# Index scores of a sparse attention in six pairs instead of four groups of three

## What is computed

```python
# per layer of the first block, z = h @ w_in + b_in, split into
#   qa, ka, va, qi, ki, wi, qb, kb, vb, ga, gb
qi = partial_rope(qi.reshape(b, s_len, 8, 64), cos, sin)      # index queries, 8 heads
ki = partial_rope(ki.reshape(b, s_len, 1, 64), cos, sin)      # one index key
# per block of 128 queries:
logits = einsum('bqhd,bsd->bqhs', qib, k_idx)
score = einsum('bqh,bqhs->bqs', wb, relu(logits)) * INDEX_SCALE
score = where(admissible, score, -inf)
_, sel = top_k(score, 128)                 # 128 keys are kept for each query
# softmax attention of qa over the chosen ka, va; beside it a banded attention of
# qb (rms-normed), kb (rms-normed), vb; then gates, projections and an FFN
```

## Time and profile before

| | |
|---|---|
| median of three runs | 3193.2 us |
| lowest, highest | 3189.02, 3198.23 us |
| profiled execution, its own time | 3192.15 us |
| its span, first to last instruction | 3190.6 us |
| mean granted TensorE clock, share of full speed | 0.979 |
| busy: TensorE, VectorE, ScalarE, GpSimd | 3015.2, 1709.6, 1261.1, 1094.2 us |
| index scores of layer 0, of layer 1 | from 97.9, from 930.7 us |
| first band score of layer 0, of layer 1 | 149.3, 982.1 us |

### The profile page before, as it was taken

How to read it: one execution, slowest core, us unless ns; L and a number is a source line. 1 busy time by engine, 2 the same in 40 slices (tenths; PEclk the granted TensorE clock), 3 DMA queues, 4 the chain that set the end, 5 groups by cost and what they waited for, 6 DMA issues and landing times.

```text
span 3190.6 us, 36918 instructions
## 1 busy us (share of the span) xinstructions
PE 3015.2 (95%) x13938; PEld 2279.8 (71%) x13938; DVE 1709.6 (54%) x2835; ACT 1261.1 (40%) x1912; POOL 1094.2 (34%) x538
## 2 busy tenths in 40 slices
PE   5999999999989999999998999999999997999998
PEld 2666777888756667788785777877777885666664
DVE  5687664222157868422214454655677136666664
ACT  4355434223245453422323444323334234455543
POOL 1242343444423324344442554444444431000001
PEclk9999999999999999999999999999999998999999
DMA  5112563433321136374232333624442334899995
GB/s 226 53 60 73 173 200 110 147 125 100 114 80 53 57 103 238 116 308 149 91 112 78 115 119 109 194 86 117 137 124 67 93 106 174 340 381 382 381 383 207
DMA packets 188505, 501.25 MB, mean 157 GB/s; under 512 B 20080, under 2 KB 98032, under 8 KB 172224
## 3 DMA queue, kind: packets, MB, share of 16 engines
q1 hardware_dynamic: 165808, 417.24, 38.5%
q0 software_dynamic: 13200, 49.32, 4.0%
q10 hardware_dynamic: 9344, 32.61, 2.9%
HBM read 463.83 MB, written 35.29 MB: 156 GB/s over the span
## 4 chain that ended last, share of the span: by engine, by line
PE 75%; DVE 12%; ACT 4%; DMA 4%; issue 2%; POOL 1%; ACTq 1%; SPq 0%; DVEq 0%; POOLq 0%
PE banks L739 18%; PE banks L740 18%; PE banks L741 18%; PE banks L1451 5%; PE banks L1432 2%; PE banks L1434 2%; PE banks L1433 2%; DMA ring<-in_w_all 2%; PE banks L832 1%; PE banks L853 1%; PE banks L842 1%; DVE abuf L2333 1%; ACT w_hi L1536 1%; PE banks L813 1%; DMA arena<-in_w_all 1%
## 5 line engine op out<-in xcount | busy, mean ns | idle before, releaser
L3012 POOL TENSOR_TENSOR w_lo<-ring,w_hi 128x1024 fp32r<-128x1024 f32 (+1 forms) x375 | 907.3, 2422 | 1385.9 <-ACT w_hi L1536 1385.9
L740 PE MATMUL banks<-h_lo,w_hi 128*128 128x512 f32 x2104 | 827.9, 393 | 0.0
L739 PE MATMUL banks<-hx_hi,w_hi 128*128 128x512 f32 (+2 forms) x1400 | 592.3, 423 | 35.8 <-DVE h_lo L2195 16.3
L1536 ACT ACTIVATE w_hi<-ring 128x1024 fp32r<-128x1024 f32 (+1 forms) x375 | 388.8, 1038 | 551.1 <-DMA ring<-in_w_all 481.5
L741 PE MATMUL banks<-hx_hi,w_lo 128*128 128x512 f32 (+2 forms) x1400 | 553.9, 396 | 0.0
L740 PEld LDWEIGHTS banks<-h_lo,w_hi 128*128 128x128 f32 x2104 | 399.5, 190 | 86.7 <-issue 10.2
L739 PEld LDWEIGHTS banks<-hx_hi,w_hi 128*128 128x128 f32 (+2 forms) x1400 | 266.8, 191 | 153.0 <-issue 81.1
L741 PEld LDWEIGHTS banks<-hx_hi,w_lo 128*128 128x128 f32 (+2 forms) x1400 | 266.2, 190 | 61.0
L739 PE MATMUL banks<-hf_hi,w_hi 128*128 128x512 f32 x704 | 274.7, 390 | 4.0 <-DVE h_lo L2195 4.0
L741 PE MATMUL banks<-hf_hi,w_lo 128*128 128x512 f32 x704 | 273.9, 389 | 0.0
L2502 DVE TENSOR_TENSOR arena<-sgs,banks 128x512 f32<-128x512 f32 x44 | 30.3, 689 | 324.8 <-PE banks L741 324.8
(11 more groups left out here) (448 smaller groups left out, 5338.8 us busy)
## 6 DMA issues: line engine op xcount, KB each, us to landing
ring<-in_w_all SPq DMA_DIRECT2D x352, 512.0 KB, 3.9
arena<-in_w_all SPq DMA_DIRECT2D x26, 2048.0 KB, 13.4
arena<-in_w_all SPq DMA_DIRECT2D x100, 512.0 KB, 4.8
ring<-in_w_all SPq DMA_DIRECT2D x46, 1024.0 KB
arena<-in_w_all SPq DMA_DIRECT2D x25, 1024.0 KB, 31.3
x<-in_w_all SPq DMA_DIRECT2D x23, 1024.0 KB, 9.7
abuf<-in_w_all SPq DMA_DIRECT2D x32, 512.0 KB, 5.3
routed<-abuf POOLq DMA_DIRECT2D x1, 12288.0 KB, 52.9
```

Of the source, the lines that this page charges most:

```text
L739: pe.matmul(bank[0:m, :], upper, hi, start=first, stop=False)
L740: pe.matmul(bank[0:m, :], upper, lo, start=False, stop=False)
L1536: act.activation(hi_at(u)[:, 0:n], raw_at(u)[:, 0:n], ACT.Copy).then_inc(w_upper, 1)
L3012: pool.tensor_tensor(lo_at(u)[:, 0:n], raw_at(u)[:, 0:n], hi_at(u)[:, 0:n], ALU.subtract)\
```

## The change

The twelve steps stay the same, with the same products, rectifications and accumulations. They are issued in six pairs (0, 1), (2, 3), ... (10, 11) in place of four groups of three. The pairs stand on TensorE behind the projections qi2, qi3, qb0, kb0, vb0 and qb1; the groups stood behind qi2, qi3, qb0 and kb0. Each step now waits by itself for its `qi`, since pairs cross from one `qi` to the next. On ScalarE and VectorE the steps are spread likewise, but 6, 7 and 8 stand together there.

```diff
-                def index_scores(j):
-                    prepared("qi%d" % j)
-                    for i in range(1, QT):
-                        n = 3 * j + i - 1
+                def index_scores(a):
+
+                    for n in (a, a + 1):
+                        j, i = n // 3, 1 + n % 3
+                        prepared("qi%d" % j)
                         step = at("mix", "ix") + n
...
                 index_scores(0)
                 rotate("qi1", raw_of("qi1"))
                 make("qi3")
-                index_scores(1)
+                index_scores(2)
                 rotate("qi2", raw_of("qi2"))
                 make("qb0")
-                index_scores(2)
+                index_scores(4)
                 rotate("qi3", raw_of("qi3"))
                 make("kb0")
                 head_norm("qb0")
-                index_scores(3)
+                index_scores(6)
                 make("vb0")
+                index_scores(8)
                 head_norm("kb0")
                 make("qb1")
+                index_scores(10)
                 turn_values(0)
...
-                rectify(0)
+                rectify(0, 1)
                 take("qi3")
-                rectify(1)
+                rectify(2, 3)
                 take("qb0")
                 square("qb0")
-                rectify(2)
+                rectify(4, 5)
                 take("kb0")
                 head_root("qb0")
                 square("kb0")
-                rectify(3)
+                rectify(6, 7, 8)
                 take("vb0")
+                rectify(9)
                 head_root("kb0")
+                rectify(10, 11)
                 take("qb1")
...
+                        if n >= 3:
+                            dve.wait_ge(sem("acc_done"), at("mix", "ix") + n - 2)
                         dve.wait_ge(sem("rl_done"), at("mix", "ix") + n + 1)
...
-                    dve.wait_ge(sem("acc_done"), at("mix", "ix") + 3 * j + 3)
...
-                accumulate(2)
+                accumulate(4, 5)
                 index_rotated(3)
+                accumulate(6, 7, 8)
                 head_normed("qb0", qT[0], v1("qn_b"), sem("prep_done"))
-                accumulate(3)
+                accumulate(9, 10, 11)
+                dve.wait_ge(sem("acc_done"), at("mix", "ix") + 12)
```

More of the change, by code:

```diff
@@ L1676, in head_root, with rectify @@
                     rough_inverse_root(at("mix", "aux") + SUMS.index("n_" + name))
-                def rectify(j):
-                    for i in range(1, QT):
-                        w, n = P * (i + 1), 3 * j + i - 1
+                def rectify(*numbers):
+                    for n in numbers:
+                        w = P * (2 + n % 3)
                         step = at("mix", "ix") + n
@@ L2336, in turn_values, with accumulate @@
                     take_transposed(sums("t_vb%d" % j), vtok[j % 2], aux.rearrange("p (a b) -> p a b", b=P))
-                def accumulate(j):
-                    for i in range(1, QT):
-                        w, n = P * (i + 1), 3 * j + i - 1
+                def accumulate(*numbers):
+                    for n in numbers:
+                        j, i = n // 3, 1 + n % 3
+                        w = P * (i + 1)
+                        if n >= 3:
+                            dve.wait_ge(sem("acc_done"), at("mix", "ix") + n - 2)
                         dve.wait_ge(sem("rl_done"), at("mix", "ix") + n + 1)
@@ L2371, in _ @@
                 index_rotated(0)
-                accumulate(0)
+                accumulate(0, 1)
                 index_rotated(1)
-                accumulate(1)
+                accumulate(2, 3)
                 index_rotated(2)
-                accumulate(2)
+                accumulate(4, 5)
                 index_rotated(3)
+                accumulate(6, 7, 8)
                 head_normed("qb0", qT[0], v1("qn_b"), sem("prep_done"))
-                accumulate(3)
+                accumulate(9, 10, 11)
+                dve.wait_ge(sem("acc_done"), at("mix", "ix") + 12)
                 mine(dve.tensor_copy(mask[:, 0, 0:P], adm[:, SEQ - P:SEQ]))
```

## The result

The change makes the kernel slower: 3198.84 us (median of 12 runs, 3193.68 to 3209.39) against 3190.43 us (12 runs, 3183.85 to 3203.67). The ratio is 1.0027, with a 95% interval from 1.0016 to 1.0038, that is +8.6 us (5.1 to 12.1). It is a loss of a quarter of a per cent, and clear of the noise. The profiled execution took 3193.68 us, its span 3192.1 us, mean granted clock 0.979 as before. It is the fastest of its twelve, while the profiled execution of the kernel before lies 1.7 us above its median, so the two spans differ by 1.5 us only. The comparison has to be made inside the stretch, and the size of the loss has to come from the medians.

A forecast was written before the change was run, and what follows sets the result against it. TensorE was taken as the chain for three quarters, with VectorE arriving together with it at the first band score. 2 x (4.5 + 1.0 for low clock) = +11.0 us on a median of 3193.2 gave 3204.2, range 3196 to 3212.

The forecast's parts named there:

- my own case: Whole kernel: VectorE's later line and lost clock make it slower, 3204.2 us, own range 3200 to 3209, chance 0.62.
- The chance of 0.66: Whole kernel: chance given to a slowdown of more than 0.3%, 9.6 us.
- All waits for a rectification go, TensorE 8 us earlier: TensorE in the index-score stretch: no wait for a rectification left, through its transposes at 141.1, 8 us earlier.
- The scores' length: TensorE's index scores: 0.63, 0.85 and 1.06 us for 256, 384 and 512 columns, putting score 8 at 130.6.
- The line from score 8 to the last accumulation: ScalarE and VectorE, through qb0's norm, take("vb0") and rectify 9: from 130.6 to 144.8, accumulations ending 6.0 us later.
- From the last accumulation to the band score: VectorE's mask, four selection rounds and kb0's norm: from 144.8 to the first band score at 153.8.
- +4.5 us a layer: First band score in each layer: 153.8 instead of 149.31, bounds 3.5 to 6.2 us.
- The clock, +1.0 a layer: TensorE after nearly 13 us idle before the band score: low clock costs 0.1 to 1.7 us a layer, 1.0 taken.
- The rival that it stays low for 12 us: TensorE in the band attention: low clock for 12 us loses 4.3 us a layer, 17.6 in all, 3211; chance 0.12.
- The shift: Behind the stretch: every engine goes on from kb0's norm in the same order and distances, so the delay reaches the end.
- rival "no change": Kinder GpSimd holds or a DMA-paced stretch behind cut the delay to 2 or 3 us a layer, about 3198; chance 0.16.
- rival "faster": TensorE's waits go and nothing replaces them, if accumulations end by about 138.8: 16.4 us less, 3177; chance 0.10.

The follow-up runs named there:

- Pairs, upper late: Changed kernel with the upper half of vb1's weight moved from behind take("vb0") to behind take("qb1"); ratio 1.0013, +4.1 us against the kernel before.
- threes last: Changed kernel with steps 6, 7, 8 behind kb0 and 9, 10, 11 behind vb0 as threes; ratio 1.0015, +4.8 us against the kernel before.
- norm late: Kernel before with VectorE making kb0's norm after eight selection rounds, not four; ratio 1.0020, +6.4 us against the kernel before.
- kept busy: Changed kernel with twelve more TensorE products, results unused, just before the first band score; ratio 1.0039, +12.5 us against the kernel before.
- nine early: Changed kernel with step 9 rectified ahead of take("vb0") and accumulated ahead of qb0's norm; ratio 1.0016, +5.1 us against the kernel before.
- uppers late: Relu first with the upper halves of kb1's and vb1's weights made later, GpSimd's lower halves following; 3183.74 us, ratio 0.9973 against the kernel before.
- Relu first: Kernel before, in threes, with a group's first two rectifications ahead of the weight's upper half, accumulations 9 and 10 before qb0's norm; ratio 0.9996, -1.3 us.

## Why the prediction was right

The direction, the mechanism and the size came as forecast: +11 us forecast, +8.6 (5.1 to 12.1) measured. The measured median of 3198.84 us lies in the stated range of 3196 to 3212, but below my own case of 3200 to 3209; the kernel before had a median of 3190.43 beside it and not 3193.2, which makes 2.8 us of that. The chance of 0.66 stood on a loss of over 0.3%. The measured 0.27% lies just under that line, with an interval (0.16% to 0.38%) that reaches over it, so this part of the forecast is not borne out. Step by step:

- *All waits for a rectification go, TensorE 8 us earlier.* Right: 0.2 us a layer of them is left, and TensorE was through at 140.4 us (141.1 forecast).
- *The scores' length.* Too large. Score 8 came at 129.55 and not at 130.6, and 0.17 of this is the layer's start. I had added up rows of one score with their ends (0.63, 0.85, 1.06); from the start of a pair to the next row it is 1.28 (97.69 to 98.97) where my sum has 1.48. Over eight scores I counted 0.8 us too much.
- *The line from score 8 to the last accumulation.* Right. Forecast 14.2 us (130.6 to 144.8), measured 14.5 (129.55 to 144.02), with each link where it was put: norm of `qb0` behind accumulation 8, `take("vb0")` behind the norm, GpSimd begun before accumulation 9 (138.10 against 138.62), 5.40 us for the six passes. "Pairs, upper late" takes one link out and gives back 1.3 us; "threes last" puts score 8 ahead of `vb0` and gives back 2.6. These two, and "norm late", which makes the loss out of the late norm alone, show the cause.
- *From the last accumulation to the band score.* 9.0 forecast, 9.05 measured (144.02 to 153.07).
- *+4.5 us a layer.* 3.9 measured. The scores were 0.8 us shorter than in my sum and the line behind them 0.3 longer, so the two errors partly cancel.
- *The clock, +1.0 a layer.* 0.9 and 1.2, from "kept busy" against the change. After a wait of 12.7 us the matmuls start every 0.43 us until 158.24, that is 1.2 GHz for 5.2 us; in layer 1 it is 6.0 us (988.41 to 994.42). The rival that it stays low for 12 us is refuted by the row at 158.77. That my 1.0 came true is partly luck, since it was the middle between two rows with short waits. The trace of the kernel before has a wait of nearly the same length that I had overlooked, at the start of layer 0:

```profile
53.50 0.77 PE L739 MATMUL banks<-hx_hi,w_hi 128*128 128x512 f32 x1 [12.03 <-DVE h_lo L2195]
...
57.04 0.40 PE L741 MATMUL banks<-hx_hi,w_lo 128*128 128x512 f32 x1
```

Behind it the clock was low for 3.5 us. By my own working that makes 3.5 x 0.47 - 1.35 = 0.3 us a layer, an estimate that would have been further off. The rule of the Trainium skill that the prediction names (it stands in that page's section "Why this matters for your kernels") held for the long gap: the clock was lost, in both layers. The granted clock by stretch (busy time of the engines, then PEclk, DMA share and GB/s) after the change:

```profile
153.00:159.00 6.00, 5.93 (x17) 4.60 (x18) 4.86 (x17) 2.62 (x6) 2.38 (x1) 0.55 0.00 1
159.00:165.00 6.00, 6.00 (x26) 3.50 (x25) 3.92 (x10) 4.71 (x13) 0.07 (x1) 1.00 0.11 16
```

- *The shift* (by how much a profile is later than that of before at the same place) *is carried to the end.* By the medians, mostly: 10.0 us are made in the two stretches (4.8 and 5.2 at 813) and 8.6 arrive. By the two profiled executions it is not so clean. The profile of the change is 6.0 us behind that of before at 897, then only 2.3 at 931, where layer 1's stretch begins, 9.1 at 1102, and falls from 7.8 at 1708 to 1.5 at the end, in a layer that the change does not touch. The fall around 907 has rows. TensorE before, then after the change:

```profile
907.53 2.08 PE L813 MATMUL banks<-arena,cst 128*128 128x512 f32 x2 [3.98 <-DVEq L300]
```

```profile
910.69 1.13 PE L813 MATMUL banks<-arena,cst 128*128 128x512 f32 x2 [1.12 <-DVEq L300]
```

Both end a chain that starts at a load of a weight. ScalarE before, then after:

```profile
901.13 1.06 ACT L1536 ACTIVATE w_hi<-ring 128x1024 fp32r<-128x1024 f32 x1 [3.76 <-DMA ring<-in_w_all]
```

```profile
904.10 1.06 ACT L1539 ACTIVATE w_hi<-ring 128x1024 fp32r<-128x1024 f32 x1 [0.69 <-DMA ring<-in_w_all]
```

Before, ScalarE stood 3.76 us for that load; after the change it came later and stood 0.69. This is the taking up that the rival "no change" names. But in the profiles of norm late and nine early the delay is the same before and behind that place to within 0.3 us (norm late 5.9 at 897, 5.8 at 924) with waits of TensorE of 3.7 and 3.8 us there as in before. In all nine kernels of the experiments that wait is between 2.4 and 3.8 us, and only the change's profile has 1.12, so it depends on how that load fell in one execution. Whether it takes a part of the loss in most runs stays open; the medians allow for 0 to 5 us. The third layer's drift is open too, and it is not the change's own: from 1708 to the end the ten profiles gain or lose between -6.8 and +2.6 us against before, in code that is the same.

The rival "faster" fell as foreseen, since the accumulations ended at 144 and not by 138.8. Its condition was the right one: "uppers late" meets it (mask begun 36.8 us after the layer's first score, before 41.0), and is faster. "Relu first" meets it too (38.50), but loses 2.1 us again in the hold at the mask, and its gain of 2.1 us at 813 over both layers does not show in its time. What I had not seen is that the condition can be met with the groups of three kept.

## What to carry to other kernels

When two engines arrive together at a join (here within 0.3 us), removing the waits of one buys nothing; look at what sets the other, and count for each moved step what stands behind it on the engine that takes it over. Spreading work more evenly for one engine can put the last piece later, as it did here, and the last piece is what the next stage waits for. Where a short operation of ScalarE (a rectification) frees a bank and a long one (preparing a later weight) has time, change their order before changing the order of TensorE; and put GpSimd's elementwise work where VectorE runs instructions that it was seen not to hold, here the search for maxima and their replacement.

## What the runs showed of the hardware

GpSimd's lower half of a weight (two inputs, 128x1024, 2.35 to 2.6 us) holds VectorE's instructions of two inputs in SBUF that come while it runs. Six passes of the accumulation took 5.40 us for 3.70, three instructions of the mask 3.88 for 1.74, the first step of a norm 1.49 for 0.69: 0.8 to 2.1 us each time. The search for a maximum and the replacement kept 0.43 and 0.41 us under the same instruction ("uppers late", 136.23 to 138.62).

That one input is enough to be safe would be wrong. The first pass of all accumulations (line 2345) multiplies one tensor by a column of weights and adds nothing. In the kernel before it meets a lower half on GpSimd:

```profile
100.12 2.06 DVE L2345 TENSOR_SCALAR arena<-abuf,arena 128x256 f32<-128x256 f32 x1 [3.47 <-ACT abuf L1685]
```

```profile
99.67 2.35 POOL L3012 TENSOR_TENSOR w_lo<-ring,w_hi 128x1024 fp32r<-128x1024 f32 x1 [3.58 <-ACT w_hi L1536]
```

In "relu first" it comes ahead of that lower half (100.70) and takes 0.35 us:

```profile
98.86 0.35 DVE L2345 TENSOR_SCALAR arena<-abuf,arena 128x256 f32<-128x256 f32 x1 [2.59 <-ACT abuf L1686]
```

The Trainium skill (SBUF — State Buffer, Who interferes with whom) has this rule: a VectorE instruction with two inputs in SBUF contends with a GpSimd instruction that reads it, and one with at most one input there does not, unless it runs in a mode that takes both of VectorE's ports; `tensor_scalar` is among those that it says can. The rows agree on the two inputs and on the two selection instructions, and the held `TENSOR_SCALAR` is the exception by its time; no run here shows in which mode it ran. Moving two lower halves away from the norm and the mask is 2.9 of the 3.9 us a layer between "relu first" and "uppers late" at the band score.

The low clock after the long wait was cheap. A wait of 12.7 us was followed by 5.2 us at 1.2 GHz, of which 0.9 to 1.2 us remained at the next join; one of 12.03 us at the start of layer 0 had been followed by 3.5 us, and one of 2.22 us by 6.4 us. In "threes last" a wait of 2.96 us kept full clock in layer 0, and one of 2.95 us at the same place in layer 1 was followed by 6.0 us at 1.2 GHz, which put the band score 2.85 us later. The length of the wait did not set the length of what followed, and here a short wait cost more than the long one, since `take("vb0")` and the last accumulations hang on the projection that ran behind it.
